# Two modulation slabs in the arena, and small loads, the attention bias, the first output slab and the first transposes moved, in a two-layer block kernel on one core

## The chip, the cores and the metric

The kernel runs on one core of one Trainium2 chip. The metric is the device time of one execution in microseconds (us); the median of the timed runs counts. The profile is one further execution with the hardware profiler. PE is TensorE, DVE is VectorE, ACT is ScalarE, POOL is GpSimd; SyncE (SP) computes nothing and only issues transfers.

## The reference, cut to what matters

The input is a sequence of 256 tokens of 1024 features, float32. Two blocks follow each other.

```
mod = silu(c) @ ada_w + ada_b                     # six rows: shift1, scale1, gate1, shift2, scale2, gate2
h = rms_norm(x, norm_mix_w) * (1 + scale1) + shift1
proj = h @ w_in                                   # attention q, k, v; gated scan q, forget, value, gate; branch gates
x = x + gate1 * ((g0 * (att @ w_branch_att) + g1 * (scan @ w_branch_hg)) @ w_out)
h = rms_norm(x, norm_ffn_w) * (1 + scale2) + shift2
x = x + gate2 * expert_choice_ffn(h)              # 16 experts, 32 tokens each, 1024 x 2048 gate, up and down
# second block: gMLP with spatial gating, squared-ReLU MLP, banded attention with a
# relative bias per head, squared-ReLU MLP
```

## The kernel before, in words

The work is one long hand-written program for each engine, and the engines meet only through semaphores. Weights come in slabs of 2 MB. `FIRST_SLABS` lists the 27 slabs of the stage before the experts in the order in which SyncE issues them: `ada0` to `ada11` are column blocks of the modulation weight, `W0` to `W10` of `w_in`, `att`, `hg`, `out0` and `out1` the branch and output weights. They go round a ring of three slots (`slot_of`, `BEFORE`, line 484 issues them), and a slot is loaded again when the slab three places earlier has been used: for an `ada` slab when TensorE has finished its job, for the others when VectorE has written the low part of its last chunk (`chunk_low`). The 192 expert slabs, 16 KB to each partition, go round six slots; the second three lie where `parts` lay, so they wait for the last product before the experts.

Most products are made in three passes over a high and a low part of both operands. ACT copies a chunk (half a slab) to its rounded high part (line 701), DVE subtracts to get the low part (line 1117, both called by `split_to`), and three chunk buffers are used in turn. `ada` slabs are multiplied as they are: `ada_part` (line 1848) makes four partial rows, DVE copies them out (line 1168), and `ada_col` (line 1858) or `ada_row` (line 1869) sums and turns them. DVE makes `modc` and `aff1` from them (line 1220).

`JOBS` is the order in which TensorE fills PSUM: job i uses bank pair i modulo 4 and waits until job i - 4 has been drained. `norm(0)` transposes the normalised input (line 1760, jobs `nT0a`, `nT0b`). Then `turn_out` scales and shifts it: ACT writes the high part in four quarters (line 743), DVE recomputes each quarter into `tmp`, of which there are two halves (line 1161), and POOL subtracts to get the low part (line 592, `low_parts`). TensorE waits for all four low parts and for the first chunk of `W1`, and starts the projections (lines 1777 to 1779).

At the end of the mixer stage TensorE computes `ya`, `yh` (the branches), `ada10`, the transposes `mT` of the merged rows, `mo0` with `out0`, the row of `ada10`, `ada11`, and `mo1` with `out1`. `mo0` and `mo1` have 48 matrix products each, in two halves of 24. POOL loads the attention bias of the second block (2 MB, line 650) once `yh1` is done. The arena is 64 KB of each partition (`at(kb, columns)`); its first 32 KB are unused until `W1` has been computed.

Before the first slab, SyncE, ACT and POOL issue thirteen small loads for the vectors (lines 490, 491, 492, 688, 574), ACT then `x` and before all of them the constants, and POOL the router weight and three weight rows (lines 578 to 583). SyncE waits for all small vectors before the second slab:

```python
if n == 1:
    sp.wait_ge(vrow_in, 16 * 10)
    sp.wait_ge(vrow_in2, 16 * 3)
```

## Time and profile before

| | us |
|---|---|
| median of 3 timed runs | 1966.03 (1964.84 to 1968.62) |
| the profiled execution, its own time | 1967.66 |
| its span in the trace | 1965.8 |
| chain that ended last: DMA, PE, DVE, ACT | 44%, 43%, 7%, 3% |
| PE busy, DVE busy, ACT busy, POOL busy | 1441.2, 594.1, 487.7, 107.4 |
| transfers, mean | 287 GB/s, 565.12 MB |

An engine's busy time says how much it worked, not what it was worth. The chain that ended last is followed back from the last instruction, at each step to what released it; only what lies on it moves the end. A granted clock of 1.00 is 2.4 GHz and of 0.50 is 1.2 GHz.

### The profile page before, as it was taken

Reading aid. Unit: us, or ns where it says so; the run is one execution under the profiler, and the core shown is the slowest. Engines: PE = TensorE matmul, PEld = TensorE weight load, DVE = VectorE, ACT = ScalarE, POOL = GpSimd, SP = SyncE. Lnnn points to the kernel's source line nnn. Section 1 sums busy time; section 2 is a strip of 40 time slices with the busy share of each in tenths; the row PEclk is TensorE's granted clock in tenths of the full one; section 3 lists DMA queues with packets and bytes.
Section 4 is the critical chain, followed back from the end, with each engine's and each line's share of the span. In section 5 each row is a group of like instructions: output and inputs, shape, how many; then the busy total and the mean of one; then the engine's idle time right before and its main releaser. Section 6 shows DMA issues by size and latency. Waiting matters only on the chain.

```text
span 1965.8 us, 19906 instructions
## 1 busy us (share of the span) xinstructions
PE 1441.2 (73%) x8303; PEld 871.5 (44%) x8303; DVE 594.1 (30%) x677; ACT 487.7 (25%) x636; POOL 107.4 (5%) x93
## 2 busy tenths in 40 slices
PE   4868798666566566566566556559799989879998
PEld 2865576311111111111111111118598879668987
DVE  2475655300000000000000000026545545655554
ACT  3443452200000000000000000034434444544343
POOL 2453200200000000000000000000000000000000
PEclk8978899688877888878878888869799999989999
DMA  9422577499999999999999999985245434314450
GB/s 334 152 86 86 199 252 262 177 428 430 428 428 430 427 428 429 428 428 429 428 428 429 428 428 429 428 341 189 79 180 201 176 129 172 136 57 172 173 198 36
DMA packets 97432, 565.12 MB, mean 287 GB/s; under 512 B 4732, under 2 KB 5896, under 8 KB 72808
## 3 DMA queue, kind: packets, MB, share of 16 engines
q1 hardware_dynamic: 94792, 555.81, 70.0%
q0 software_dynamic: 2112, 7.06, 1.2%
q10 hardware_dynamic: 480, 1.57, 0.2%
q8 instruction: 35, 0.57, 0.1%
q14 instruction: 13, 0.11, 0.0%
HBM read 563.37 MB, written 1.05 MB: 287 GB/s over the span
## 4 chain that ended last, share of the span: by engine, by line
DMA 44%; PE 43%; DVE 7%; ACT 3%; issue 2%; POOL 1%; SPq 0%; DVEq 0%; ACTq 0%; POOLq 0%
DMA ring_b<-in_w_exp_down_dram 22%; DMA ring_b<-in_w_exp_up_dram 20%; PE PS L1777 11%; PE PS L1778 11%; PE PS L1779 11%; PE PS L2080 3%; PE PS L2094 2%; PE PS L1760 1%; DMA ring_a<-in_ada_w_dram 1%; PE PS L1910 1%; DMA ring_a<-in_w_out_dram 1%; DVE parts L1117 1%; DMA ring_a<-in_w_in_dram 1%; DVE arena L1234 1%; POOL hT L592 1%
## 5 line engine op out<-in xcount | busy, mean ns | idle before, releaser
L2080 PE MATMUL PS<-ring_a,arena 128*32 128x512 f32 x1280 | 188.6, 719 | 120.0 <-DMA ring_a<-in_w_exp_up_dram 69.7
L2080 PE MATMUL PS<-ring_b,arena 128*32 128x512 f32 x768 | 128.2, 802 | 98.9 <-DMA ring_b<-in_w_exp_up_dram 63.3
L1777 PE MATMUL PS<-hT,parts 128*128 128x256 f32 x672 | 193.1, 287 | 10.2 <-POOL hT L592 8.0
L2094 PE MATMUL PS<-ring_b,arena 128*32 128x512 f32 x768 | 124.0, 777 | 98.1 <-DMA ring_b<-in_w_exp_down_dram 98.0
L1778 PE MATMUL PS<-hT,parts 128*128 128x256 f32 x672 | 192.4, 286 | 0.0
L1779 PE MATMUL PS<-hT,parts 128*128 128x256 f32 x672 | 192.2, 286 | 0.0
L1506 DVE TENSOR_TENSOR arena<-PS,arena 128x512 f32<-128x512 f32 x16 | 11.1, 692 | 597.5 <-PE PS L2080 597.5
L1117 DVE TENSOR_TENSOR parts<-ring_a,parts 128x2048 fp32r<-128x2048 f32 (+1 forms) x62 | 141.6, 2292 | 110.0 <-ACT parts L701 109.8
L1626 DVE TENSOR_TENSOR parts<-ring_a,parts 128x2048 fp32r<-128x2048 f32 x60 | 137.4, 2292 | 107.4 <-ACT parts L1009 106.8
L2080 PEld LDWEIGHTS PS<-ring_a,arena 128*32 128x32 f32 x1280 | 37.6, 120 | 261.2 <-DMA ring_a<-in_w_exp_up_dram 110.8
L701 ACT ACTIVATE parts<-ring_a 128x2048 fp32r<-128x2048 f32 (+1 forms) x62 | 116.6, 1890 | 142.2 <-PE PS L1779 107.9
L1009 ACT ACTIVATE parts<-ring_a 128x2048 fp32r<-128x2048 f32 x60 | 114.7, 1912 | 114.6 <-PE PS L1779 114.6
L1777 PEld LDWEIGHTS PS<-hT,parts 128*128 128x128 f32 x672 | 131.3, 195 | 13.2 <-POOL hT L592 8.4
L1778 PEld LDWEIGHTS PS<-hT,parts 128*128 128x128 f32 x672 | 131.3, 195 | 0.5
L1779 PEld LDWEIGHTS PS<-hT,parts 128*128 128x128 f32 x672 | 131.3, 195 | 0.0
L1779 PE MATMUL PS<-parts,rounded 128*128 128x512 f32 x320 | 126.8, 396 | 0.0
L1778 PE MATMUL PS<-parts,rounded 128*128 128x512 f32 x320 | 126.8, 396 | 0.0
L1777 PE MATMUL PS<-parts,rounded 128*128 128x512 f32 x320 | 126.8, 396 | 0.0
L1777 PE MATMUL PS<-parts,hT 128*128 128x512 f32 (+1 forms) x288 | 116.2, 403 | 10.9 <-issue 7.1
L1778 PE MATMUL PS<-parts,hT 128*128 128x512 f32 (+1 forms) x288 | 114.3, 397 | 0.0
L2080 PEld LDWEIGHTS PS<-ring_b,arena 128*32 128x32 f32 x768 | 24.2, 128 | 202.5 <-DMA ring_b<-in_w_exp_up_dram 104.0
L1779 PE MATMUL PS<-parts,hT 128*128 128x512 f32 (+1 forms) x288 | 113.8, 395 | 0.0
(284 smaller groups left out, 1651.1 us busy)
## 6 DMA issues: line engine op xcount, KB each, us to landing
ring_a<-in_w_exp_gate_dram SPq DMA_DIRECT2D x48, 2048.0 KB, 25.8
ring_b<-in_w_exp_down_dram SPq DMA_DIRECT2D x48, 2048.0 KB, 26.2
ring_b<-in_w_exp_up_dram SPq DMA_DIRECT2D x32, 2048.0 KB, 26.2
ring_a<-in_w_exp_up_dram SPq DMA_DIRECT2D x32, 2048.0 KB, 25.6
ring_b<-in_w_exp_gate_dram SPq DMA_DIRECT2D x16, 2048.0 KB, 27.1
ring_a<-in_w_exp_down_dram SPq DMA_DIRECT2D x16, 2048.0 KB, 26.6
ring_a<-in_w_up_dram SPq DMA_DIRECT2D x16, 2048.0 KB, 8.6
ring_a<-in_w_down_dram SPq DMA_DIRECT2D x16, 2048.0 KB, 7.6
```

The source lines that it names most:

```text
L592: pool.tensor_tensor(low, tmp[:, b * NB:(b + 1) * NB], high.bitcast(F32), ALU.subtract)\
L701: act.activation(part_of(c, 0), raw(c), ACT.Copy).then_inc(chunk_high, 1)
L1009: act.activation(part_of(c, 0), raw(c), ACT.Copy).then_inc(chunk_high, 1)
L1117: dve.tensor_tensor(part_of(c, 1), raw(c), part_of(c, 0).bitcast(F32), ALU.subtract)\
L1234: dve.tensor_tensor(split(dst, s)[side], split(dst, s)[side], split(src, s)[side], ALU.mult)
L1626: dve.tensor_tensor(part_of(c, 1), raw(c), part_of(c, 0).bitcast(F32), ALU.subtract)\
L1760: ins = nc.tensor.transpose(bank(job, i // 4)[:, (i % 4) * P:(i % 4 + 1) * P], src, ident)
L1777: mm(out, left[0], right[0], start=start, stop=False)
L1778: mm(out, left[0], right[1], start=False, stop=False)
L1779: return mm(out, left[1], right[0], start=False, stop=stop)
L2080: ins = mm(PS[32 * j:32 * j + 32, side, :], xe[:, 2 * q + kk, :], w[:, kk, j * NB:(j + 1) * NB], start=q == 0 and kk == 0, stop=q == 3 and ...
L2094: ins = mm(PS[32 * q:32 * q + 32, 2 + n, :], hidT[:, q, 32 * i:32 * i + 32], w[:, q, n * NB:(n + 1) * NB], start=i == 0, stop=i == 3)
```

## The change

`ada0` and `ada1` get two slots of their own in the arena, and the ring of three starts with `ada2`; so the first five slabs are issued one behind the other, and SyncE no longer waits for the small vectors. ACT loads the identity first (64 KB) and the rest of the constants (425 KB) after `x`, with two semaphores in place of one. POOL issues the router weight and the three weight rows after the low parts of `nT0`. TensorE makes `adc1` and `adc2` earlier and the transposes `norm(0)` before `ada3`. ACT and DVE split the first chunk of `W1` after the turn-out of `nT0` and not before it, and the forget-gate bounds are computed after the first norm. `out0` is loaded before `ada10`; `ada11` is computed right behind `ada10`, before the transposes `mT`. The attention bias is loaded after the experts, behind the first of four norm rows.

```diff
--- before.py
+++ after.py
@@ -46,15 +46,15 @@
...
     [("vecT", 1)]
-    + [(j, 1) for j in ("ada0", "ada1", "adc0", "ada2", "adc1", "ada3", "adc2", "adc3")]
-    + [("nT0a", 2), ("nT0b", 2)]
+    + [(j, 1) for j in ("ada0", "ada1", "adc0", "adc1", "ada2", "adc2")]
+    + [("nT0a", 2), ("nT0b", 2), ("ada3", 1), ("adc3", 1)]
     + [("W1", 2), ("W2", 2), ("W0", 2), ("lv0", 2), ("W4", 2), ("lv1", 2), ("W5", 2), ("lv2", 2), ("W3", 2)]
...
     + [("adr4", 1), ("adr5", 1), ("ohgT", 2), ("W9", 2), ("W10", 2), ("ya0", 2), ("ya1", 2), ("yh0", 2), ("yh1", 2)]
-    + [("ada10", 1), ("mTa", 2), ("mTb", 2), ("mo0", 2), ("adr10", 1), ("ada11", 1), ("mo1", 2), ("adr11", 1)]
+    + [("ada10", 1), ("ada11", 1), ("mTa", 2), ("mTb", 2), ("mo0", 2), ("adr10", 1), ("mo1", 2), ("adr11", 1)]
     + [("nT1a", 2), ("nT1b", 2), ("rt", 1), ("rl", 1), ("aT", 1), ("ic", 1), ("ib", 1)]
@@ -75,7 +75,7 @@
...
     + [("ada4", "ada4"), ("ada5", "ada5"), ("W9", "W9"), ("W10", "W10"), ("att", "ya1"), ("hg", "yh1")]
-    + [("ada10", "ada10"), ("out0", "mo0"), ("ada11", "ada11"), ("out1", "mo1")]
+    + [("out0", "mo0"), ("ada10", "ada10"), ("ada11", "ada11"), ("out1", "mo1")]
 )
@@ -134,13 +134,15 @@
...
+    if n < 2:
+        return R + n
     if n < AT_EXPERT:
-        return n % RS
+        return (n - 2) % RS
     return (n - AT_EXPERT) % R if n < AT_A else (n - AT_A) % RS
-ARRIVED, BEFORE, _count, _last = [], [], [0] * R, [None] * R
+ARRIVED, BEFORE, _count, _last = [], [], [0] * (R + 2), [None] * (R + 2)
 for _n in range(AT_FFN[1] + 2 * FJ):
@@ -290,13 +292,14 @@
...
         psum_drained = [sem(f"psum_drained{i}") for i in range(4)]
-        slab_in = [sem(f"slab_in{i}") for i in range(R)]
+        slab_in = [sem(f"slab_in{i}") for i in range(R + 2)]
         chunk_high, chunk_low = sem("chunk_high"), sem("chunk_low")
...
         slab_done = sem("slab_done")
-        consts_in, x_in, rows_in, wr_in = (sem(n) for n in ("consts_in", "x_in", "rows_in", "wr_in"))
+        ident_in, tables_in, x_in, rows_in, wr_in = (
+            sem(n) for n in ("ident_in", "tables_in", "x_in", "rows_in", "wr_in"))
@@ -359,6 +362,8 @@
...
             i = slot_of(n)
+            if i >= R:
+                return at(16 * (i - R), SLOT)
             return ring_a[:, i, :] if i < RS else ring_b[:, i - RS, :]
@@ -493,10 +498,6 @@
...
                 n = SLAB_AT[name]
-                if n == 1:
-
-                    sp.wait_ge(vrow_in, 16 * 10)
-                    sp.wait_ge(vrow_in2, 16 * 3)
                 if name.startswith("ada"):
@@ -574,14 +575,6 @@
...
             link(pool.memset(wr[:, :, :], 0.0))
-            for a in range(2):
-                pool.dma_start(wr.rearrange("p (q a) e -> p q a e", a=2)[:, :, a, 0:NE],
-                               A["w_router"][0].rearrange("(q p a) e -> p q a e", p=P, a=2)[:, :, a]).then_inc(wr_in, 16)
-
-            pool.dma_start(wqk[:, 0:64], A["q_norm_w"][0].partition_broadcast(P)).then_inc(rows_in, 16)
-            pool.dma_start(wqk[:, 64:128], A["k_norm_w"][0].partition_broadcast(P)).then_inc(rows_in, 16)
-            pool.dma_start(hgw[:, :], A["hg_norm_w"][0].partition_broadcast(P)).then_inc(rows_in, 16)
-
             def low_parts(jobs):
@@ -593,6 +586,14 @@
...
             low_parts(("nT0a", "nT0b"))
+
+            for a in range(2):
+                pool.dma_start(wr.rearrange("p (q a) e -> p q a e", a=2)[:, :, a, 0:NE],
+                               A["w_router"][0].rearrange("(q p a) e -> p q a e", p=P, a=2)[:, :, a]).then_inc(wr_in, 16)
+
+            pool.dma_start(wqk[:, 0:64], A["q_norm_w"][0].partition_broadcast(P)).then_inc(rows_in, 16)
+            pool.dma_start(wqk[:, 64:128], A["k_norm_w"][0].partition_broadcast(P)).then_inc(rows_in, 16)
+            pool.dma_start(hgw[:, :], A["hg_norm_w"][0].partition_broadcast(P)).then_inc(rows_in, 16)
@@ -627,6 +628,7 @@
             pool.wait_ge(rows_in, 48)
+            pool.wait_ge(tables_in, 16)
             pool.wait_ge(qk_rstd, 1)
@@ -645,12 +647,6 @@
...
-
-            wait_full(pool, "yh1")
-            pool.dma_start(bias[:, :, :], hankel(A["b_rel_bias_2"])).then_inc(bias_in, 16)
-            pool.wait_ge(bias_in, 16)
-
-            pool.memset(bias[0:64, :, 0:64], NEG).then_inc(bias_masked, 1)
@@ -679,14 +675,19 @@
...
                 pool.dma_start(grows[n], row.partition_broadcast(P)).then_inc(grow_in[n % 2], 16)
+                if n == 0:
+                    pool.dma_start(bias[:, :, :], hankel(A["b_rel_bias_2"])).then_inc(bias_in, 16)
+                    pool.wait_ge(bias_in, 16)
+                    pool.memset(bias[0:64, :, 0:64], NEG).then_inc(bias_masked, 1)
...
         def _(act):
-            act.dma_start(consts[:, :], A["consts"]).then_inc(consts_in, 16)
+            act.dma_start(ident, A["consts"][:, C_ID:C_ID + P]).then_inc(ident_in, 16)
             for v, src in VECTORS[4:8]:
...
             act.dma_start(x[:, :, :], A["x"][0].rearrange("(t p) d -> p t d", p=P)).then_inc(x_in, 16)
+            act.dma_start(consts[:, P:C_END], A["consts"][:, P:C_END]).then_inc(tables_in, 16)
@@ -751,14 +752,13 @@
...
             act.wait_ge(lb_in, 1)
-            act.activation(small[:, 24:32], small[:, 16:24], ACT.Exp).then_inc(lb_exp, 1)
             act.activation(csil[:, :], vcol[:, V_C:V_C + 8], ACT.Silu).then_inc(c_silu, 1)
...
                 root(0, t)
-            split_to(0)
+            act.activation(small[:, 24:32], small[:, 16:24], ACT.Exp).then_inc(lb_exp, 1)
             act.wait_ge(aff_ready, 1)
@@ -1197,30 +1197,29 @@
...
             ins.then_inc(crep_ready, 1)
+            for t in range(T):
+                mean_square(0, t)
+            for t in range(T):
+                rescale(0, t)
             dve.wait_ge(lb_exp, 1)
...
             dve.tensor_scalar(small[:, 8:16], small[:, 0:8], -1.0, 1.0, ALU.mult, ALU.add).then_inc(lb_ready, 1)
-            for t in range(T):
-                mean_square(0, t)
-            for t in range(T):
-                rescale(0, t)
             ada_part(0)
...
             ada_col(0)
+            ada_col(1)
             ada_part(2)
-            ada_col(1)
+            ada_col(2)
             ada_part(3)
-            ada_col(2)
             ada_col(3)
...
             dve.wait_ge(aff_ready, 1)
-            split_to(0)
             turn_out(("nT0a", "nT0b"), aff1, modc)
@@ -1256,6 +1255,7 @@
...
             dve.tensor_tensor(EK, gkf, gkb, ALU.add).then_inc(factors_ready, 1)
+            dve.wait_ge(tables_in, 16)
             scores(0)
@@ -1413,6 +1413,7 @@
...
             ada_part(10)
+            ada_part(11)
             wait_drained(dve, "adc9")
@@ -1431,7 +1432,6 @@
...
             ada_row(10, gate2[:, 0:NB])
-            ada_part(11)
@@ -1868,7 +1868,7 @@
...
-            pe.wait_ge(consts_in, 16)
+            pe.wait_ge(ident_in, 16)
             pe.wait_ge(vrow_in, 16 * 10)
@@ -1881,12 +1881,12 @@
...
             ada_col(0)
+            ada_col(1)
             ada_part(2)
-            ada_col(1)
+            ada_col(2)
+            norm(0)
             ada_part(3)
-            ada_col(2)
             ada_col(3)
-            norm(0)
             pe.wait_ge(low_out, 4)
@@ -1998,13 +1998,13 @@
...
             ada_part(10)
+            ada_part(11)
             pe.wait_ge(merged_ready, 4)
...
             ada_row(10)
-            ada_part(11)
             natural_by_tile("mo1", hT)
@@ -2021,6 +2021,7 @@
...
             wait_drained(pe, "rt")
+            pe.wait_ge(tables_in, 16)
             for t in range(T):
```

## Rows read from the trace of the kernel before

**Rows 1.** Chain in order of time, expert stage: start, length (us), what, count.

```profile
385.43 10.48 PE PS L2080 x96
...
1274.47 27.41 DMA ring_b<-in_w_exp_down_dram
```

**Rows 2.** Timeline, 0 to 60 us, all engines.

```profile
11.44 0.61 ACT L713 ACTIVATE junk<-x 128x512 bf16<-128x512 f32 x1
...
17.20 0.72 ACT L722 ACTIVATE xn<-x,rstd 128x512 f32<-128x512 f32 x1 [0.23 <-DVE rstd L1130]
...
25.33 1.05 PE L1858 MATMUL PS<-mean,arena 128*128 128x1 f32 x8
...
28.99 3.41 PE L1848 MATMUL PS<-ring_a,crep 128*32 128x512 f32 x16 [2.60 <-DMA ring_a<-in_ada_w_dram]
...
34.41 2.67 PE L1848 MATMUL PS<-ring_a,crep 128*32 128x512 f32 x16 [1.03 <-DMA ring_a<-in_ada_w_dram]
...
37.01 3.58 PE L1858 MATMUL PS<-mean,arena 128*128 128x1 f32 x16
37.13 0.69 DVE L1168 COPY arena<-PS 128x512 f32<-128x512 f32 x1 [3.54 <-PE PS L1848]
...
40.45 3.65 PE L1760 MATMUL PS<-consts,xn 128*128 128x128 f32 x16
...
40.82 0.17 DVE L1220 SCALAR_TENSOR_TENSOR aff<-modc,vcol 128x8 f32<-128x8 f32 x1
...
42.49 3.75 ACT L743 ACTIVATE hT<-PS,modc,aff 128x256 fp32r<-128x256 f32 x8 [0.86 <-PE PS L1760]
43.95 1.90 DVE L1161 TENSOR_SCALAR tmp<-PS,aff,modc 128x256 f32<-128x256 f32 x4
```

**Rows 3.** Chain in order of time, around 52 us.

```profile
52.08 0.58 PE PS L1777
```

**Rows 4.** Busy time by stretch; last columns granted clock, DMA share, GB/s.

```profile
9.00:15.00 6.00, 0.00 (x0) 0.00 (x0) 1.92 (x16) 5.85 (x13) 0.00 (x0) 1.00 1.00 186
20.00:25.00 5.00, 3.31 (x28) 0.47 (x20) 0.69 (x1) 0.00 (x0) 0.00 (x0) 1.00 1.05 387
330.00:332.00 2.00, 2.00 (x6) 1.58 (x5) 1.97 (x5) 0.72 (x2) 0.00 (x0) 0.50 1.01 434
...
1325.00:1330.00 5.00, 2.98 (x7) 2.46 (x8) 4.95 (x7) 2.75 (x4) 0.00 (x0) 0.50 0.00 0
```

**Rows 5.** DMA queues, 10 to 15 us: packets, MB, share of 16 engines.

```profile
q0 software_dynamic: 84, 0.11, 55.3%
```

**Rows 6.** GpSimd's subtractions of line 592: duration ns min/median/max, first and last start.

```profile
L592 POOL TENSOR_TENSOR hT<-tmp,hT x4: 1261/1262/3303, 45.0 to 48.7; 128x512 fp32r<-128x512 f32 x4
```

**Rows 7.** VectorE's low parts, line 1117, 48 to 54 us, same columns.

```profile
L1117 DVE TENSOR_TENSOR parts<-ring_a,parts x2: 2361/2852/3344, 48.5 to 50.8; 128x2048 fp32r<-128x2048 f32 x2
```

**Rows 8.** GpSimd's timeline.

```profile
67.84 2.16 POOL L603 TENSOR_SCALAR arena<-arena,small 128x256 f32<-128x256 f32 x4 [15.82 <-ACT arena L772]
```

**Rows 9.** Timeline of PE, 304 to 343 us.

```profile
305.54 1.92 PE L1848 MATMUL PS<-ring_a,crep 128*32 128x512 f32 x16
308.32 1.97 PE L1760 MATMUL PS<-consts,xn 128*128 128x128 f32 x16 [0.86 <-DVE xn L1412]
312.67 0.47 PE L1777 MATMUL PS<-parts,hT 128*128 128x512 f32 x1 [2.38 <-issue]
...
323.67 1.03 PE L1869 MATMUL PS<-arena,mean 128*128 128x512 f32 x2
...
328.96 0.73 PE L1777 MATMUL PS<-parts,hT 128*128 128x512 f32 x1 [2.41 <-DVE parts L1117]
...
341.54 1.02 PE L1869 MATMUL PS<-arena,mean 128*128 128x512 f32 x2
```

**Rows 10.** Chain in order of time, 305 to 330 us.

```profile
307.52 14.83 DMA ring_a<-in_w_out_dram
```

**Rows 11.** DMA issues, 305 to 340 us: count, KB each, us to landing.

```profile
arena<-in_b_rel_bias_dram POOLq DMA_DIRECT2D x1, 2048.0 KB, 12.6
```

## The prediction

> **What bounds the kernel now.** I read the page first: its chain is 44% transfers and 43% TensorE, so there are stages with different limits. The chain in order of time separates them. From 385.43 us, when TensorE opens the first expert, to 1301.88 us (1274.47 + 27.41) each step is the arrival of an expert slab [rows 1]: a stream of fixed length, 916.4 us, that starts when TensorE frees the first slot. Behind it lie 663.9 us to the end of the span, which the change touches at one place only. So a microsecond won before 385.43 is one won at the end, and what counts is the chain before it. There it is led by TensorE and its partners, with two stretches in which a transfer sets the pace: the start, up to `W1`'s first product at 52.08 [rows 3], where the timeline of all engines shows TensorE taking each modulation slab as it lands [rows 2]; and `out1`, for which the chain waits 14.83 us from 307.52 [rows 10]. The change works on these two.
>
> **The start, part one: when the slabs land.** From 20 to 25 us the transfers run at 387 GB/s, from 9 to 15 us at 186 [rows 4]. That is 6.0 x (387 - 186) = 1206 KB less, or 3.1 us at 387. In 10 to 15 us POOL's queue has 84 packets of 0.11 MB but 55.3% of the engines' time [rows 5]; these are the router weight and the three rows, which now leave this window. Their 0.2 MB gives another 0.5 us. Sum 3.6 us: `ada2`, taken at 28.99 [rows 2], then lands at 25.4. The bounds are 0 (the hole has another cause) and 3.6. The missing wait of SyncE before `ada1`, the two arena slots and the earlier issues are costed at nothing: the transfer engines are full from 20 us on, so a deeper queue moves no byte sooner. The constants bring the same bytes in another order.
>
> **Part two: TensorE from `ada2` to `aff1`.** Before, `aff1` is written at 40.82 + 0.17 = 40.99 [rows 2], after `ada3` (34.41), its copy, and `adc2` with `adc3` (3.58 for both). Now TensorE does, from 25.4: `ada2`, copy, `adc2`, 16 transposes, `ada3`, copy, `adc3`, and DVE's sum and `aff1`. An `ada` part took 3.41 and 2.67 here [rows 2] and 1.92 later [rows 9]; one column job 1.05 or 3.58 / 2 = 1.79; the transposes 3.65 here and 1.97 later; a copy 0.69, 0.75 with its hand-overs [rows 2]; the last two 0.35. These pairs are the two levels of TensorE's clock, and it was changing between them here, so I take the middle: 2.67 + 0.75 + 1.4 + 2.8 + 2.67 + 0.75 + 1.4 + 0.35 = 12.8, hence 38.2. All fast gives 9.8 (35.2), all slow 3.41 + 0.75 + 1.79 + 3.65 + 3.41 + 0.75 + 1.79 + 0.35 = 15.9 (41.3). The transposes stand in front of `ada3` and delay it beyond its landing at 30.8; that price is in the sum. The normalised input was complete at 17.92 [rows 2], so they don't wait for it.
>
> **Part three: from `aff1` to `W1`.** Before this takes 52.08 - 40.99 = 11.1. ACT started its turn-out at 42.49, released by the transposes; these are now done, so it starts 0.07 behind `aff1` and saves 1.4. Its first quarter was done at 42.49 + 3.75 / 4 = 43.43, and DVE began only at 43.95 [rows 2], behind the low part of `W1`'s first chunk; that split is moved, so 0.5 more goes. What remains is 11.1 - 1.9 = 9.2. But the moved split meets POOL's last quarter: three of POOL's subtractions took 1.26 us and the one beside DVE's split 3.30 [rows 6], while of DVE's two splits the first took 2.36 and the second 3.34 [rows 7]: each waited for the other's whole instruction. Before, a split lay there too, so the 9.2 holds it: DVE finishes the turn-out 5.7 behind ACT's start, and then 2.36 of split and 1.26 of POOL stand in a row in either order, ending at 9.2 to 9.4. The Trainium skill has this as a rule that speaks against moving the split (SBUF — State Buffer, on the shared port pair): the pair is an exclusive lock, and the second of the two engines fully blocks. By that rule the trace agrees; without a lock the stage would take 8.1, 1.1 less. `W1` then starts at 38.2 + 9.2 = 47.4, a gain of 4.7 (7.7 all fast, 1.6 all slow; with no earlier landings 1.1 in the middle and -2.0 all slow).
>
> Other edits at the start cost nothing: the exponential for the forget bounds and DVE's four steps of it are due at POOL's work at 67.84, before which POOL idled 15.82 [rows 8]; the same gap covers the five issues on POOL, and SyncE's queue isn't behind them. The waits for the rest of the constants come long after these land. If the gap were gone, POOL's issues would cost 3 us. From 52 to 305 us the order is unchanged and the chain passes through no transfer, so the gain is carried whole; a microsecond may be lost where POOL and DVE meet otherwise.
>
> **The end of the mixer stage** (times as before, unshifted). TensorE makes `ada10` from 305.54 and the transposes `mT` from 308.32. With `ada11` (1.92) behind `ada10` they start at 305.54 + 2 x 1.9 = 309.35, 1.03 later. `mo0` moves from 312.67 to 313.70 and its row job from 323.67 to 324.70; then comes `mo1`, 1.0 later, at 325.7, where before it started at 328.96 [rows 9]. It took 12.58 (to 341.54), `mo0` 11.00 for the same 48 products; the granted clock was 0.50 in 330 to 332 [rows 4], after TensorE had waited 2.41. Without that wait I take 11.00, so `mo1` ends at 336.7, 4.8 us earlier.
>
> Is `out1` there in time? It now waits for the low part of `out0`'s last chunk (written at 304.9, as before) and not for `ada10`, which gives 2.6. It was in flight for 14.83 [rows 10], beside the bias, 2 MB in 12.6 [rows 11]. Even at 14.83 it lands at 319.7. Both halves, high and low, took from 322.35 to 328.96, 6.6: ready at 326.3, and `mo1` would start 0.6 later. I take no delay, since the bias is gone. The second half of `out1` waits for a chunk buffer that `mo0`'s first half frees at 313.70 + 5.5 = 319.2; one half of the 6.6 less DVE's other split is 4.2, ready at 323.4, under 325.7. Gain 4.8; bounds 3.3 (clock low as before) and 4.8. The expert slabs behind `out1` have some 50 us to land.
>
> **The bias, now behind the experts.** POOL issues it near 1318 us; at 12.6 it lands by 1331, and the transfer engines moved nothing from 1325 to 1330 [rows 4]. The slab after that is used tens of us later and the bias at 1696. POOL's mask is one memset of 1 us; it could block one split on DVE, at most 1 us, with no one waiting. Cost 0, upper bound 1.
>
> **Sum.** 4.7 + 4.8 = 9.5 us. The profiled execution had 1965.8 of span and 1967.66 in all; it becomes 1956.3 of span and 1958.2. It lay 1.6 above the median of 1966.03, so the median becomes 1956.5.
>
> **Rivals.**
> 1. *The start gives little.* The hole at 9 to 15 us isn't POOL's traffic, or the clock stays low through the transposes. The start gives 1.1 to 1.6, the sum is 6.1, the time 1959.9. For it: the granted clock fell in this stretch before, and half of the hole has few POOL packets. Against: the queue's 55.3%.
> 2. *The start at full clock.* TensorE has less idle between its jobs; 7.7 + 4.8 = 12.5, the time 1953.5.
> 3. *`mo1` gains little:* `out1` is late for another reason, 4.8 becomes 1, the time 1960.3. Against it stand the 2.3 us of slack.
> 4. *Slower: `x` arrives behind the five slabs.* The old order kept `ada1` back until the small vectors were in. If the transfer engines now serve five queued slabs before ACT's queue, `x` lands with `W1`, near 36; its norm took 6.5 (11.44 to 17.92 [rows 2]), and then 16 transposes at 2.8, `ada3` 2.67, copy, `adc3` and 0.35 put `aff1` at 50.5 and `W1` at 59.7: 7.6 later, less 4.8, so 2.8 slower net, 1968.8; with the clock low as well, up to 1972. The transposes wait from the point at which `x` lands after 24; the start's gain is gone at 28, and the kernel is slower from 33. Against: `x` was here by 11.44 beside a queued slab.
>
> The Trainium skill has a rule on this (DMA: Bandwidth & Descriptors, on queues, rings and completion order): each transfer engine goes round-robin over the queues it has work for. By that rule this rival does not happen; no run here has shown five slabs queued.
>
> **How the numbers follow.** Forecast (start 3 to 6.5, end 3.3 to 4.8) 0.57; rival 1 0.20; rival 2 0.10; rival 3 0.07; rival 4 and unforeseen waits 0.06. The range reaches to rival 2 and past rival 1: 1952.8 to 1961.5. A change within 0.2% (3.9 us) is what a measurement can't tell from none. Faster by more: all of the forecast and rival 2, most of 1 and 3, 0.89; the same 0.07; slower 0.04.
>
> **What would show it.** The new profile should have the modulation slabs taken near 14.5, 20 and 25.4; no 186 GB/s in 9 to 15; transposes ahead of the last `ada` part; one long POOL subtraction still; `W1` from 45 to 50; no wait for `out1` ahead of `mo1`, about 11 us for `mo1`; the first expert near 375.9; the slab stream still 916 us; nothing waiting on POOL near 1320. The prediction is wrong if the stream's length changes, if the gain of the start is eaten between 52 and 305, or if the hole stays.

## The result and the profile after

The changed kernel takes 1953.07 us in the median of 9 runs, against 1966.03 in 9 runs of the kernel before: ratio 0.9933, 95% interval 0.9915 to 0.995. Timed again later it gave 1958.36 (6 runs) against 1967.76, ratio 0.9948, interval 0.9935 to 0.996. By the ratios the change is worth 10.2 and 13.2 us, by the medians 9.4 and 13.0, where 9.5 (a time of 1956.5) was forecast; the median of all 15 runs of the changed kernel is 1955.49. The profiled execution took 1949.28 with a span of 1947.5. It is 3.8 us under the median, and the one of before was 1.6 over; the difference of 18.3 us between the two traces is therefore more than the change gives, and part of this study is to say which of it is the change.

The timeline of the changed kernel's first 50 us (start, length, engine, line, output and input) answers to [rows 2 and 3]. The slabs `ada0` to `ada3` are multiplied at 14.57, 19.89, 25.54 and 31.13:

```profile
8.97 0.63 ACT L714 ACTIVATE junk<-x 128x512 bf16<-128x512 f32 x1 [0.78 <-DMA x<-in_x_dram]
...
14.57 3.64 PE L1848 MATMUL PS<-arena,crep 128*32 128x512 f32 x16 [8.78 <-DMA arena<-in_ada_w_dram]
...
19.89 3.64 PE L1848 MATMUL PS<-arena,crep 128*32 128x512 f32 x16 [1.67 <-DMA arena<-in_ada_w_dram]
...
25.54 1.92 PE L1848 MATMUL PS<-ring_a,crep 128*32 128x512 f32 x16
...
29.25 1.95 PE L1760 MATMUL PS<-consts,xn 128*128 128x128 f32 x16
...
31.13 1.92 PE L1848 MATMUL PS<-ring_a,crep 128*32 128x512 f32 x16
...
35.21 0.17 DVE L1220 SCALAR_TENSOR_TENSOR aff<-modc,vcol 128x8 f32<-128x8 f32 x1
35.41 3.76 ACT L744 ACTIVATE hT<-PS,modc,aff 128x256 fp32r<-128x256 f32 x8 [18.43 <-DVE aff L1220]
...
44.75 0.58 PE L1777 MATMUL PS<-hT,parts 128*128 128x256 f32 x1 [9.78 <-POOL hT L585]
```

Four things are to be seen here: `ada2` is multiplied 3.5 us earlier than in [rows 2]; the transposes (line 1760) stand ahead of the last `ada` part and take the short duration; the turn-out is released by `aff1` itself, 0.03 behind it; and `x` is in time, at 8.97. The busy time in 9 to 15 us (granted clock, DMA share and GB/s last) shows the hole filled, against [rows 4]:

```profile
9.00:15.00 6.00, 0.43 (x4) 0.23 (x8) 1.70 (x8) 5.42 (x13) 0.00 (x0) 1.00 1.04 390
```

One caution for reading the granted clock: that column says 1.00 from the start of the span, also while TensorE is idle, and it still says 1.00 while `ada0` and `ada1` take 3.64, the duration that goes with 0.50 elsewhere (u2's `ada2`: 3.64 at 0.50). Ahead of the first fall in a profile, the durations tell the level and the column does not.

The instructions of GpSimd's and VectorE's lines in the same stretch (minimum, median, maximum in ns), as in [rows 6 and 7]:

```profile
L585 POOL TENSOR_TENSOR hT<-tmp,hT x4: 1260/1264/3316, 37.7 to 41.4; 128x512 fp32r<-128x512 f32 x4
```

```profile
L1117 DVE TENSOR_TENSOR parts<-ring_a,parts x3: 2278/2369/3357, 41.2 to 46.8; 128x2048 fp32r<-128x2048 f32 x3
```

One of four subtractions is long and so is one of three splits, as before. At the end of the mixer stage TensorE's timeline answers to [rows 9]: both `ada` parts together (x32), and `mo1` right behind the row job of `ada10`.

```profile
297.56 3.64 PE L1848 MATMUL PS<-ring_a,crep 128*32 128x512 f32 x32
...
316.48 1.02 PE L1869 MATMUL PS<-arena,mean 128*128 128x512 f32 x2
316.94 0.79 PE L1777 MATMUL PS<-parts,hT 128*128 128x512 f32 x1
...
328.27 1.02 PE L1869 MATMUL PS<-arena,mean 128*128 128x512 f32 x2
```

And the chain in order of time, for the expert stage [rows 1]:

```profile
370.88 12.18 PE PS L2081 x96
...
1262.15 25.63 DMA ring_b<-in_w_exp_down_dram
```

The stream of slabs takes 916.9 us (to 1287.78), against 916.4. Set beside each other, in us:

| stretch | before | after | difference |
|---|---|---|---|
| start to `W1` | 52.08 | 44.75 | -7.3 |
| `W1` to `ada10` | 253.5 | 252.8 | -0.7 |
| `ada10` to the end of `mo1` | 36.0 | 30.7 | -5.3 |
| end of `mo1` to the first expert | 43.9 | 42.6 | -1.3 |
| slab stream | 916.4 | 916.9 | +0.5 |
| last expert slab to the end | 663.9 | 659.7 | -4.2 |

The two stretches on which the change works give 12.6. The other rows differ as much between executions of kernels that are alike there, as the experiments show. In the row from `mo1` to the first expert this is again TensorE's clock: it is 42.6 to 42.7 in the six profiles with the new end in which the 16 transposes of the second norm take 2.2, and 44.7 in the three (e3, u3, c1) in which they take 3.69.

### The profile page after: what moved, and what is told of

It reads as the page before. It is cut to its first block, busy times and chain, and to the rows that moved or that the text cites. A ratio compares the mean times of both kernels' runs of the same rounds, so it can differ in the third digit from the quotient of the medians.

```text
span 1947.5 us, 19908 instructions
## 1 busy us (share of the span) xinstructions
PE 1440.6 (74%) x8303; PEld 865.2 (44%) x8303; DVE 594.5 (31%) x677; ACT 488.2 (25%) x636; POOL 107.3 (6%) x93
## 4 chain that ended last, share of the span: by engine, by line
PE 45%; DMA 43%; DVE 7%; ACT 3%; issue 2%; POOL 1%; SPq 0%; DVEq 0%; ACTq 0%; POOLq 0%
DMA ring_b<-in_w_exp_down_dram 21%; DMA ring_b<-in_w_exp_up_dram 20%; PE PS L1777 11%; PE PS L1778 11%; PE PS L1779 11%; PE PS L2081 3%; PE PS L2095 2%; PE PS L1760 1%; DMA arena<-in_ada_w_dram 1%; PE PS L1910 1%; PE PS L1848 1%; DVE arena L1233 1%; POOL hT L585 1%; DVE arena L1234 1%; ACT junk L714 0%
## 5 line engine op out<-in xcount | busy, mean ns | idle before, releaser
L2081 PE MATMUL PS<-ring_b,arena 128*32 128x512 f32 x768 | 130.6, 816 | 101.2 <-DMA ring_b<-in_w_exp_up_dram 64.8
L2095 PE MATMUL PS<-ring_b,arena 128*32 128x512 f32 x768 | 129.6, 809 | 92.0 <-DMA ring_b<-in_w_exp_down_dram 91.9
L1506 DVE TENSOR_TENSOR arena<-PS,arena 128x512 f32<-128x512 f32 x16 | 11.1, 691 | 596.4 <-PE PS L2081 596.4
L2081 PEld LDWEIGHTS PS<-ring_a,arena 128*32 128x32 f32 x1280 | 38.2, 122 | 256.6 <-DMA ring_a<-in_w_exp_up_dram 105.4
L1777 PEld LDWEIGHTS PS<-hT,parts 128*128 128x128 f32 x672 | 131.0, 195 | 14.7 <-POOL hT L585 9.9
L1777 PE MATMUL PS<-parts,hT 128*128 128x512 f32 (+1 forms) x288 | 114.4, 397 | 8.4 <-issue 7.1
L2081 PEld LDWEIGHTS PS<-ring_b,arena 128*32 128x32 f32 x768 | 24.4, 130 | 205.1 <-DMA ring_b<-in_w_exp_up_dram 105.2
L2095 PEld LDWEIGHTS PS<-ring_b,arena 128*32 128x32 f32 x768 | 24.2, 130 | 199.1 <-DMA ring_b<-in_w_exp_down_dram 155.8
L1778 PE MATMUL PS<-parts,hT 128*128 128x512 f32 (+1 forms) x288 | 112.6, 391 | 0.0
```

What stands on the lines that cost most here:

```text
L1777: mm(out, left[0], right[0], start=start, stop=False)
L1778: mm(out, left[0], right[1], start=False, stop=False)
L2081: ins = mm(PS[32 * j:32 * j + 32, side, :], xe[:, 2 * q + kk, :], w[:, kk, j * NB:(j + 1) * NB], start=q == 0 and kk == 0, stop=q == 3 and ...
L2095: ins = mm(PS[32 * q:32 * q + 32, 2 + n, :], hidT[:, q, 32 * i:32 * i + 32], w[:, q, n * NB:(n + 1) * NB], start=i == 0, stop=i == 3)
```

## The experiments

Four kernels carry one part of the change each on the kernel before (e1 to e4), five undo one part of it or its order in the changed kernel (u1 to u5), one is the changed kernel again (c1), and two try something further (k1, k2). Each was timed in several rounds beside the kernel before and profiled once. The table has the milestones of the profiles (us) and the ratio of the times to the kernel before, with its interval. The `ada2` column is the start of its products, `aff1` the end of its write, and `W1` the first product.

| kernel | `ada2` | `aff1` | `W1` | `W1` to `ada10` | `ada10` to end of `mo1` | last slab to end | ratio |
|---|---|---|---|---|---|---|---|
| before | 28.99 | 40.99 | 52.08 | 253.5 | 36.0 | 663.9 | 1 |
| e1, GpSimd's loads late | 24.98 | 37.96 | 48.71 | 256.1 | 34.3 | 659.8 | 0.9986 (0.9977 to 0.9994) |
| e2, order of the start and split | 29.80 | 44.10 | 53.39 | 256.3 | 34.2 | 659.9 | 0.9989 (0.9978 to 1.0) |
| e3, order of the end | 29.71 | 39.39 | 52.81 | 253.6 | 30.7 | 661.5 | 0.9964 (0.995 to 0.9978) |
| e4, bias late | 29.78 | 41.86 | 52.9 | 253.4 | 32.0 | 657.7 | 0.9978 (0.9967 to 0.999) |
| after | 25.54 | 35.38 | 44.75 | 252.8 | 30.7 | 659.7 | 0.9933 (0.9915 to 0.995) |
| u1, GpSimd's loads early | 30.53 | 41.66 | 50.96 | 255.9 | 30.7 | 662.6 | 0.996 (0.9943 to 0.9977) |
| u2, bias early | 25.33 | 39.18 | 48.55 | 252.9 | 30.7 | 659.1 | 0.9939 (0.9921 to 0.9956) |
| u3, split first | 25.36 | 35.19 | 49.87 | 253.8 | 30.7 | 658.5 | 0.996 (0.9941 to 0.9978) |
| u4, no arena slots | 25.33 | 36.46 | 45.82 | 255.8 | 30.7 | 662.7 | 0.9938 (0.9918 to 0.9958) |
| u5, old order of the start | 25.43 | 37.56 | 48.39 | 253.5 | 30.7 | 656.3 | 0.9937 (0.9924 to 0.995) |
| c1, the changed kernel again | 25.40 | 39.69 | 49.05 | 253.9 | 30.7 | 661.5 | 0.9948 (0.9935 to 0.996) |
| k1, TensorE kept busy, start | 26.48 | 40.22 | 55.75 | 253.4 | 30.7 | 659.5 | 0.997 (0.9957 to 0.9983) |
| k2, the same at six places | 26.70 | 38.21 | 53.75 | 253.4 | 30.7 | 664.5 | 0.9991 (0.9983 to 1.0) |

**e1: GpSimd's four loads behind the low parts, in the kernel before.**

```diff
             link(pool.memset(wr[:, :, :], 0.0))
-            for a in range(2):
-                pool.dma_start(wr..., A["w_router"]...).then_inc(wr_in, 16)
-            pool.dma_start(wqk[:, 0:64], ...); pool.dma_start(wqk[:, 64:128], ...); pool.dma_start(hgw[:, :], ...)
...
             low_parts(("nT0a", "nT0b"))
+            (the same loads)
```

> The kernel before with one part of the change: GpSimd issues the router weight and the three weight rows behind the low parts of nT0. Theory (the traffic of these four loads makes the hole of 186 GB/s in 9 to 15 us): the hole is filled, ada2 is taken near 25.5 instead of 28.99, W1's first product comes 3 to 4 us earlier, near 48.5, and the time falls by 3 to 4 us. Rival (the hole comes from SyncE's wait for the small vectors before ada1, which is kept here): the hole stays, ada2 is taken at 29, the time is unchanged.

The hole is gone while SyncE's wait before `ada1` is still there; busy time by stretch in e1:

```profile
9.00:15.00 6.00, 0.85 (x5) 0.26 (x9) 1.92 (x16) 5.85 (x13) 0.00 (x0) 1.00 1.05 392
```

`ada2` is taken at 24.98, 4.0 us before [rows 2], and `W1` starts 3.4 earlier, at 48.71. The median falls by 4.0 us (1964.37 against 1968.38), by the ratio of the runs 2.8 (1.2 to 4.5). The rival, that the wait makes the hole, is out.

**u1: the same loads early, in the changed kernel.** 

```diff
             link(pool.memset(wr[:, :, :], 0.0))
+            (the loads of wr, wqk and hgw, as in the kernel before)
...
             low_parts(("nT0a", "nT0b"))
-            (the same loads)
```

> The changed kernel with the router weight and the three weight rows issued at the start again, as in the kernel before. Theory: the hole is back although SyncE doesn't wait for the vectors, ada2 lands 3 to 3.6 us later than in the changed kernel, W1 starts near 48.5 instead of 44.75. Rival (the hole was SyncE's wait or the order of the constants): the slabs land as in the changed kernel, W1 at 45.

The hole is back without SyncE's wait, and with it GpSimd's queue; the stretches and the queues from 10 to 15 us in u1:

```profile
9.00:15.00 6.00, 0.00 (x0) 0.00 (x0) 1.35 (x7) 5.20 (x12) 0.00 (x0) 1.00 0.97 159
```

```profile
q0 software_dynamic: 94, 0.13, 61.4%
q1 hardware_dynamic: 193, 0.40, 26.6%
```

`ada2` is at 30.53 and `W1` at 50.96. The median is 1960.15, beside 1953.09 and 1953.64 for u2 and u4 in the same rounds. The first slab is multiplied at 19.69, 1.5 us later than in the kernel before too, so the loss is 5 us of landing, not 3.6. Both directions agree: these 0.2 MB of loads put the slabs off by 4 to 5 us. In this stretch a packet of GpSimd's queue held a transfer engine for 0.52 us (an estimate: 61.4% of 16 engines in 5 us, over 94 packets) and one of SyncE's queue for 0.11. Whether that comes from the small pieces of the router weight, from the broadcast of the three rows or from GpSimd's queue as such was not tried. The Trainium skill (DMA: Bandwidth & Descriptors, Queues, rings and completion order) has each transfer engine go round the queues that have work, a whole packet at a time; by that rule the small loads get turns although slabs are queued ahead of them, and the trace agrees: GpSimd's queue moved 94 packets beside 193 of SyncE's. Why a turn with so few bytes is so long, the rule doesn't say and no run here shows.

**e2: the new order of the start and the late split, in the kernel before.**

```diff
-    + [(j, 1) for j in ("ada0", "ada1", "adc0", "ada2", "adc1", "ada3", "adc2", "adc3")]
-    + [("nT0a", 2), ("nT0b", 2)]
+    + [(j, 1) for j in ("ada0", "ada1", "adc0", "adc1", "ada2", "adc2")]
+    + [("nT0a", 2), ("nT0b", 2), ("ada3", 1), ("adc3", 1)]
...
-            split_to(0)
             act.wait_ge(aff_ready, 1)
...
-            split_to(0)
             turn_out(("nT0a", "nT0b"), aff1, modc)
```

> The kernel before with the new order of TensorE and VectorE at the start (adc1, adc2 and the transposes ahead of ada3) and the first split behind the turn-out; loads as before. Theory: slabs are taken at the same times as before, aff1 stands near 38 to 40.5 by the clock, the turn-out starts at once behind it, from aff1 to W1 takes 9.2 to 9.4 instead of 11.1, W1 starts at 47.5 to 50, and the time falls by 2 to 4.5 us. Rival (the transposes ahead of ada3 cost what they save): aff1 is at or beyond 41, W1 at 50.3 or later, the time falls by less than 2.

In the profile this is a miss: `aff1` at 44.10 and `W1` at 53.39, later than before. TensorE's timeline in e2 shows why:

```profile
29.80 2.77 PE L1846 MATMUL PS<-ring_a,crep 128*32 128x512 f32 x16 [0.17 <-DMA ring_a<-in_ada_w_dram]
33.45 1.84 PE L1856 MATMUL PS<-mean,arena 128*128 128x1 f32 x8 [0.88 <-DVE arena L1167]
35.15 3.65 PE L1758 MATMUL PS<-consts,xn 128*128 128x128 f32 x16
38.74 3.02 PE L1846 MATMUL PS<-ring_a,crep 128*32 128x512 f32 x16
```

The column job took 1.84 and the transposes 3.65, so `ada3`, landed near 35, began at 38.74. The granted clock was 0.62 in 30 to 33 and 0.50 in 33 to 39. From `aff1` to `W1` it took 9.3, as forecast. So this profile shows what the rival said. Over the timed executions the part is worth 2.2 us by the ratio, and the interval (0 to 4.3) holds both the expectation and the rival: the times don't decide between them.

**u5: TensorE's and VectorE's old order, in the changed kernel** (the split stays late).

```diff
+            ada_part(2)
             ada_col(1)
-            ada_part(2)
+            ada_part(3)
             ada_col(2)
-            norm(0)
-            ada_part(3)
             ada_col(3)
+            norm(0)
```

> The changed kernel with TensorE's and VectorE's old order at the start (transposes behind ada3 and its columns, adc1 and adc2 late), the loads and the late split as in the changed kernel. Theory: ada3 is taken when it lands, 30.8; aff1 is at 34.5 to 36, not later than in the changed kernel, but the turn-out waits for the transposes and starts 1.0 to 2.5 us behind aff1; W1 at 45.5 to 47.5, the time 0.5 to 2 us above the changed kernel. Rival (the early transposes are worth what they were costed at, 1.4 us and more): W1 at 47.5 or later.

`aff1` at 37.56, the turn-out 1.50 behind it, `W1` at 48.39, beyond the 47.5 of the rival; but `ada2`, `ada3` and the transposes ran at 3.34, 2.80 and 3.65 here. The turn-out in u5, released by PE:

```profile
37.39 0.17 DVE L1220 SCALAR_TENSOR_TENSOR aff<-modc,vcol 128x8 f32<-128x8 f32 x1
39.06 3.76 ACT L744 ACTIVATE hT<-PS,modc,aff 128x256 fp32r<-128x256 f32 x8 [22.12 <-PE PS L1760]
```

The ratio is 0.9937, that of the changed kernel. The early transposes take 1.5 us off the way from `aff1` to `W1`, and they put `ada3` back: TensorE began it at 30.85 in u5, and in the kernels with the new order and the same slabs at 30.93 and 31.13 (u3 and the changed kernel, clock at 1.00 throughout) to 34.60 and 34.92 (c1 and u2, where the clock was at 0.50 ahead of it). What they save is thus lost again where the clock is low. Timed, they are worth nothing that shows.

**u3: the first split ahead of the turn-out again, in the changed kernel.**

```diff
+            split_to(0)
             act.wait_ge(aff_ready, 1)
...
+            split_to(0)
             turn_out(("nT0a", "nT0b"), aff1, modc)
```

> The changed kernel with the first split of W1 ahead of the turn-out again on ScalarE and VectorE. W1's slab landed near 43 minus the split in the changed kernel, at about 36. Theory: ScalarE waits for W1 (about 36.3), splits 1.9, and the turn-out starts at 38.2 instead of 35.4, VectorE's share of the split 2.3 ends at 40.5, so W1's first product is 3 to 3.5 us later, 48. Rival (VectorE's split in GpSimd's way costs as much as it saves): W1 within 1 us of 44.75.

The timeline of u3 from `aff1` on:

```profile
35.02 0.17 DVE L1221 SCALAR_TENSOR_TENSOR aff<-modc,vcol 128x8 f32<-128x8 f32 x1
37.45 1.91 ACT L702 ACTIVATE parts<-ring_a 128x2048 fp32r<-128x2048 f32 x1 [20.38 <-DMA ring_a<-in_w_in_dram]
39.26 3.75 ACT L744 ACTIVATE hT<-PS,modc,aff 128x256 fp32r<-128x256 f32 x8
39.46 2.29 DVE L1118 TENSOR_TENSOR parts<-ring_a,parts 128x2048 fp32r<-128x2048 f32 x1 [4.27 <-ACT parts L702]
```

ACT waits for `W1` to land, 37.4, then splits, and the turn-out starts 4.1 behind `aff1`. `W1`'s first product is at 49.87, 14.7 behind `aff1`, against 9.4 in the changed kernel: 5.3 us, more than the 3.5 expected, because DVE's half of the split comes on top (1.2). The median is 1957.38, 4 us above u2 and u4 in the same rounds, and the ratio, 0.996 against 0.9933 and 0.9948, points to 2.4 to 5.3 us; but the intervals of these kernels touch, so it is the trace that shows this part and not the time alone.

The same wait was there in the kernel before. Its chain in order of time, from `ada1` on, passes not through TensorE and `aff1` but through the landing of `W1` and its split:

```profile
25.46 14.23 DMA ring_a<-in_w_in_dram
...
39.72 1.92 ACT parts L701
...
41.74 2.29 DVE parts L1117
44.03 0.92 DVE tmp L1161 x2
```

From the start of ACT's split to `W1`'s first product it took 12.36 us here (39.72 to 52.08), 12.36 in e3 (from 40.45), 12.35 in e4 (from 40.51) and 12.42 in u3 (from 37.45), although `aff1` was anywhere from 2.3 us ahead of the split's start (u3) to 1.4 behind it (e4). Only in e1, where the transposes ran at the low clock and held the turn-out to 39.47, it took 13.0. With the split in front, the landing of `W1` thus sets the start, or the transposes come within 0.6 us of doing so; with the split behind, `aff1` does.

**u4: no arena slots, and SyncE's wait back, in the changed kernel.**

```diff
-    if n < 2:
-        return R + n
     if n < AT_EXPERT:
-        return (n - 2) % RS
+        return n % RS
...
+                if n == 1:
+                    sp.wait_ge(vrow_in, 16 * 10)
+                    sp.wait_ge(vrow_in2, 16 * 3)
```

> The changed kernel with the ring of three for all slabs and SyncE's wait for the vectors, so without the arena slots. Theory (the transfer engines are the limit, a deeper queue moves no byte sooner): the slabs are taken at the same times within 0.5 us, W1 starts at 44.8 to 45.5, the time is that of the changed kernel. Rival (the two more slots let ada3 and W1 be issued in time): ada3 or W1 lands 1 us or more later and the start loses it.

The slabs are taken at 14.49, 19.82 and 25.33, as with the slots, `W1` at 45.82, and the median is 1953.64 (ratio 0.9938). The slots are worth nothing. They do let SyncE issue sooner: `ada3` at 10.69 in the changed kernel and at 18.05 in u4, `W1` at 16.26 and at 21.81. But the slabs land at the same times. These are the transfers of `W1` in the changed kernel and in u4, from issue to landing:

```profile
ring_a<-in_w_in_dram SPq DMA_DIRECT2D x1, 2048.0 KB, 21.3
```

```profile
ring_a<-in_w_in_dram SPq DMA_DIRECT2D x1, 2048.0 KB, 15.6
```

`W1` lands at 37.6 and 37.4, and `ada3` at 30.7 in both (10.69 + 20.0 and 18.05 + 12.6). The transfer engines are busy throughout (390 and 393 GB/s in 9 to 15 us, 387 in 20 to 25), so an earlier issue only waits longer, as the prediction had it. Part of that wait is on SyncE itself. In the changed kernel the third slab's issue took 6.62 us and the fourth's 5.53; `ada3`'s took 0.37 in u4.

```profile
4.03 6.62 SPq L489 DMA_DIRECT2D ring_a<-in_ada_w_dram  x1
```

**e3: the order of the end, in the kernel before.**

```diff
-    + [("ada10", "ada10"), ("out0", "mo0"), ("ada11", "ada11"), ("out1", "mo1")]
+    + [("out0", "mo0"), ("ada10", "ada10"), ("ada11", "ada11"), ("out1", "mo1")]
...
             ada_part(10)
+            ada_part(11)
             pe.wait_ge(merged_ready, 4)
...
             ada_row(10)
-            ada_part(11)
```

> The kernel before with out0 loaded before ada10 and ada11 computed behind ada10; the bias stays where it was. Theory (the order is what frees mo1, the bias alone makes out1 slow): out1 is issued near 305 and lands 13 to 15 us later, mo1 starts at 325.7 to 327 instead of 328.96 and runs in 11.0 to 11.3, so it ends near 337.2 and the time falls by 4 to 4.8. Rival (the bias is what holds mo1, whatever the order): mo1 starts at 328 or later, the time falls by less than 1.5.

With the bias where it was, `ada10` to the end of `mo1` takes 30.7 instead of 36.0; the two row jobs on TensorE in e3 lie 11.79 apart:

```profile
325.35 1.02 PE L1869 MATMUL PS<-arena,mean 128*128 128x512 f32 x2
...
337.14 1.02 PE L1869 MATMUL PS<-arena,mean 128*128 128x512 f32 x2
```

`out1` took 10.7 beside the bias, which itself took 24.9. The time falls by 7.1 by the ratio; the interval, 4.3 to 9.8, holds the 5.3 of the stretch.

**e4: the bias behind the experts, in the kernel before.**

```diff
-            wait_full(pool, "yh1")
-            pool.dma_start(bias[:, :, :], hankel(A["b_rel_bias_2"])).then_inc(bias_in, 16)
-            pool.wait_ge(bias_in, 16)
-            pool.memset(bias[0:64, :, 0:64], NEG).then_inc(bias_masked, 1)
...
+                if n == 0:
+                    (the same, behind the first norm row)
```

> The kernel before with the attention bias loaded behind the experts and nothing else changed. Theory (the bias stretches out1's transfer, and ada11 stands between mo0 and mo1): out1, issued at 307.5, lands in 8 to 11 instead of 14.83, mo1 starts right behind ada11 near 326.6 and ends near 337.7, the time falls by about 4. Rival (out1's lateness comes from its issue time, not from the bias): out1 still takes 13 or more, mo1 starts at 328.5 or later, the time is unchanged. Behind the experts neither expects a wait for the bias: from the last expert slab's landing to the end within 2 us of 663.9.

`out1` lands in 7.6 in place of 14.83 and `ada10` to the end of `mo1` takes 32.0: 4.0 less, as expected.

```profile
ring_a<-in_w_out_dram SPq DMA_DIRECT2D x1, 2048.0 KB, 7.6
```

The time falls by 4.3 by the ratio (2.0 to 6.5). So the rival, that only the issue time makes `out1` late, is out: with the bias gone, `out1` lands in half the time. From the last expert slab to the end it takes 657.7, so behind the experts the bias costs nothing that shows.

**u2: the bias early again, in the changed kernel.**

```diff
+            wait_full(pool, "yh1")
+            (the load of the bias, its wait and its mask)
...
                 if n == 0:
-                    (the same)
```

> The changed kernel with the bias loaded at yh1 again. Theory (order and bias each give most of the end's gain, so undoing one loses little): out1 is issued 0.3 us behind the end of the yh products, takes 13 to 15, and mo1 starts 0 to 1.5 us later relative to ada10 than in the changed kernel. Rival (the gain of the end is the bias's): mo1 starts 3 us or more later and the time is 4 us above the changed kernel.

`ada10` to the end of `mo1` takes 30.7 as in the changed kernel, although `out1` needs 10.9 in place of 7.7; the ratio is 0.9939. With the new order there is slack for the bias, and moving it as well adds nothing that shows.

**c1: the changed kernel again.**

> The changed kernel once more, to see how one execution's stretches differ from another's. Theory (the slabs' arrivals are fixed, what varies is the level of TensorE's clock): ada2 taken at 25.3 to 25.6 as before; aff1 anywhere from 35.2 to 39.3, the later the more of ada2, adc2, the transposes and ada3 run at the double duration; from ada10's start to the end of mo1's products 30.7 again; slab stream 916 to 917.5. Rival (the arrivals vary): aff1 late together with late slabs.

The slabs are taken at the same times, within 0.15 us, up to `ada2`, and `aff1` is at 39.69, 4.3 later than in the first profile. TensorE's timeline in c1, and its stretches (PE busy first, granted clock third from the end):

```profile
19.90 3.27 PE L1848 MATMUL PS<-arena,crep 128*32 128x512 f32 x16 [1.69 <-DMA arena<-in_ada_w_dram]
...
25.40 3.04 PE L1848 MATMUL PS<-ring_a,crep 128*32 128x512 f32 x16 [0.30 <-DMA ring_a<-in_ada_w_dram]
29.32 1.84 PE L1858 MATMUL PS<-mean,arena 128*128 128x1 f32 x8 [0.88 <-DVE arena L1168]
31.02 3.65 PE L1760 MATMUL PS<-consts,xn 128*128 128x128 f32 x16
34.60 2.75 PE L1848 MATMUL PS<-ring_a,crep 128*32 128x512 f32 x16
```

```profile
26.00:27.00 1.00, 1.00 (x11) 0.27 (x4) 0.00 (x0) 0.00 (x0) 0.00 (x0) 0.54 1.06 389
...
27.00:30.00 3.00, 2.12 (x12) 0.71 (x4) 0.69 (x1) 0.00 (x0) 0.00 (x0) 0.50 1.05 384
```

27 to 30 us in the first profile of the same kernel:

```profile
27.00:30.00 3.00, 2.10 (x23) 1.67 (x16) 0.85 (x2) 0.00 (x0) 0.00 (x0) 1.00 1.05 385
```

The clock was 0.50 in one execution and 1.00 in the other, with the same slabs at the same times. `ada2`, the transposes and `ada3` took 3.04, 3.65 and 2.75 instead of 1.92, 1.95 and 1.92, and `W1` came at 49.05 instead of 44.75: 4.3 us, all of it of this kind. Ahead of the fall the two executions differ in little: in c1 `ada1` took 3.27 where the first profile has 3.64, TensorE then waited 0.30 for `ada2`, where it had no gap in the first profile, and the clock fell just after 26 us. No run shows whether these small differences decide it. The first trace was in any case a favourable one.

**k1: TensorE kept busy at the start.** If the clock falls while TensorE waits for slabs, products that nobody reads might hold it up. 50 float32 products of the identity (128 x 128) stand ahead of `ada0`, 72 behind `adc3`.

```diff
+            def warm(job, n, dst=None):
+                if job:
+                    begin(job)
+                    dst = bank(job, 0)[:, 0:P]
+                for _ in range(n):
+                    mm(dst, ident, ident, start=True, stop=True)
...
+            warm("ada0", 50)
             pe.wait_ge(crep_ready, 1)
...
             ada_col(3)
+            warm(None, 72, bank("ada3", 1)[:, 0:P])
             pe.wait_ge(low_out, 4)
```

> The changed kernel with products that nobody reads in two idle stretches of TensorE: 50 of 128 columns ahead of ada0 and 72 behind adc3, before W1. Theory (TensorE's clock level, and not the slabs, is what is left of the start's scatter): granted clock 1.00 from ada0 to the end of W1; all ada parts at 1.92, aff1 at 35.2 to 35.6; W1's first 18 products at 0.12 us and not 0.21; 1.7 us against the best execution and 2 to 4 in the median against the changed kernel. Rival (the extra products hold TensorE up or the clock falls all the same): W1 starts later than 45.5 or its first products take 0.21; the time is unchanged or higher.

A miss, first by its size. TensorE's timeline in k1:

```profile
5.55 12.61 PE L1877 MATMUL PS<-consts 128*128 128x128 f32 x100
...
18.09 1.92 PE L1848 MATMUL PS<-arena,crep 128*32 128x512 f32 x16
...
20.97 1.92 PE L1848 MATMUL PS<-arena,crep 128*32 128x512 f32 x16 [0.95 <-DMA arena<-in_ada_w_dram]
...
26.48 3.64 PE L1848 MATMUL PS<-ring_a,crep 128*32 128x512 f32 x16 [1.66 <-DMA ring_a<-in_ada_w_dram]
...
39.67 16.32 PE L1877 MATMUL PS<-consts 128*128 128x128 f32 x144
```

Each product is two records (x100 for 50) and takes 0.23 to 0.25 us. The second block therefore ran to 55.75, where `W1`, by the usual 9.3 behind `aff1` (40.22), was due at 49.5: some 6 us were lost to the block itself. The first block also held `ada0` back, from 14.57 to 18.09. It did raise the level at first: `ada0` and `ada1` took 1.92 each, where the changed kernel has 3.64. But then the clock fell all the same. After `ada0` and `ada1`, with a wait of 0.95 between them, and a wait of 1.66 behind the column jobs, it was 0.53 in 25 to 30 us:

```profile
25.00:30.00 5.00, 3.52 (x16) 0.69 (x16) 0.02 (x1) 0.00 (x0) 0.00 (x0) 0.53 1.05 386
```

Being busy without a gap from 5 to 18 us did not keep the clock at 26. `W1`'s products lay 0.12 apart from 55.95 on, but from `W1` to `ada10` it took 253.4, no less than in the changed kernel. The median is 1961.79, 3.4 above c1 in the same rounds. Whether smaller blocks closer to the work would gain was not tried.

**k2: the same, and such blocks around the norms later in the kernel.** The edit is that of k1 with `warm(...)` of 16 to 72 products ahead of and behind `norm(1)` to `norm(5)`.

> As the run before, with such products also in the idle stretches around the transposes of the five later norms (16 or 44 around norm(1), 72 and 16 around norm(2), 44 and 16 around norm(3) and norm(5), 60 and 16 around norm(4)). Theory: the 16 transposes of each norm take 1.9 us and not 3.7, and the first products behind them run at full clock; 3 to 4 us at each of norm(2) to norm(5) and 1 at norm(1), so the part behind the slab stream falls from 658 to 664 us to 645 to 650, and the time by 10 to 14 us against the changed kernel. Rival (the products delay the norm's own work, or the chip throttles): the part behind the stream stays above 655.

A miss too. The block ahead of `norm(2)` ran 16.34 us, and the transposes behind it were fast, at 1.91 where the changed kernel has 3.65:

```profile
1308.40 16.34 PE L1877 MATMUL PS<-consts 128*128 128x128 f32 x144
1324.58 1.91 PE L1760 MATMUL PS<-consts,xn 128*128 128x128 f32 x16
1326.33 3.74 PE L1877 MATMUL PS<-consts 128*128 128x128 f32 x32
```

But from the last expert slab to the next product of real work it took 30.3 us (1299.54 to 1329.86), against 23.5 in the changed kernel (1287.78 to 1311.30). The stretch grew by 6.8 us for the 1.7 us that the transposes saved; the median, 1966.11, is near that of before. None of these kernels beats the changed one; u2, u4 and u5 equal it.

## Why the prediction was right, point by point

**Where the slabs land.** 3.6 us were forecast, and both directions confirm place and cause: 25.54 instead of 28.99 in the profile, 4.0 in e1, 5.0 in u1. The removed wait and the arena slots were costed at nothing, for the reason that the transfer engines are full, and u4 shows both.

**TensorE from `ada2` to `aff1`.** 12.8 us with bounds of 9.8 and 15.9 put `aff1` at 38.2. The first profile showed the lower bound (35.38), c1 came out at 39.69. Over the profiles that leave the start's order and loads whole (after, u2, u4, c1) `aff1` is at 35.38, 39.18, 36.46 and 39.69, mean 37.7; in those with the old start (before, e3, e4) at 40.99, 39.39 and 41.86, mean 40.7. That is 3.0 of gain, where 2.8 was forecast, out of a scatter of 4 us that the bounds had right. It is the landing that gives it: `ada2` comes 4 us earlier, and the early transposes don't show in the time (u5).

**From `aff1` to `W1`.** 9.2 was forecast; it took 9.37 in the changed kernel, 9.3 in e2. One long subtraction on GpSimd (3316 ns beside 1260) and one long split on VectorE (3357 beside 2278) are there as before. The Trainium skill (SBUF — State Buffer, on the shared port pair) calls the pair an exclusive lock that is held for a whole instruction; the trace agrees with these four numbers. The term that the runs give another size is the moved split, booked at 0.5. That is what it cost in the kernel before behind the late transposes: ACT's turn-out began at 42.49, and DVE was free only at 44.03. But `W1` had landed only at 39.7 there, 1.3 ahead of `aff1`, and the chain of that trace passes through this landing and the split. The prediction took the path over TensorE and `aff1` for the one that sets the start; the two were within 0.6 us of each other. Had the split stayed in front, `aff1`'s earlier place would have gained nothing beyond the landing of `W1`, and u3 puts the moved split at 5.3 us. The new stretch of 9.2 holds no split in front of the turn-out, so its length was right; the share that each edit has in it was not. This also shows in the old stretch, which is 11.1, 13.4 and 11.0 (before, e3, e4): where `aff1` was early, it only waited longer.

**The end of the mixer stage.** 4.8 was forecast and 5.3 is in the profiles, 36.0 to 30.7. `mo1` takes 11.3 (316.94 to its row job at 328.27), where 11.0 was reckoned, and starts without a wait, 0.46 behind the row job of `ada10`, where 1.0 was reckoned. The new value is the same 30.7 in every kernel with the new order. The old one is 36.0, 34.3 and 34.2 (before, e1, e2). Before, `mo1` waited 2.4 and then ran partly at a granted clock of 0.50, 12.6 in all; in e1 it was `mo0` that ran partly at the low clock (0.59 in 312 to 316), and `mo1` waited 0.7 and took 11.0. So the part is worth 3.5 to 5.3, and 4.1 in the mean: within the bounds (3.3 to 4.8) but for the trace of before. What the forecast did not say is that its two edits cover for each other. The order alone gives all of it (e3), the bias alone 4.0 (e4), and both together no more than the order (u2).

**The bias behind the experts.** Costed at nothing; in the changed kernel it landed in 11.4 us, and the stretch behind the experts did not grow in e4 (657.7).

**The rest.** The stream stayed at its length (916.9 and, over all kernels, 916.2 to 917.4). From `W1` to `ada10` the kernels lie between 252.8 and 256.3, from the last slab to the end between 656.3 and 664.5, with no order in either that follows the edits. The 4.2 us that this last stretch lacks after the change is of that size, and its means are 660.8 with the change (after, u2, u4, c1) and 661.0 without (before, e3, e4), so it isn't credited to the change. By the means, `W1` comes at 47.0 with the change and at 52.6 without, 5.5 us where 4.7 was forecast; the end gives 4.1 where 4.8 was forecast. The sum, 9.7, lies beside the 9.5 partly because these two deviations cancel. The ratios say 10.2 and 13.2. The stretch from `mo1` to the first expert, shorter by 0.9 in the mean, is the only other one that follows; what makes up the rest was not located, and it is no larger than the scatter of these stretches.

**The rivals.** Rival 1 fails with the hole filled (e1), though its slow clock does occur (c1). Rival 2, the start at full clock from `ada2` on, is what the first profile shows, and the first median, 1953.07, is nearer to its 1953.5, given a chance of 0.10, than to the forecast's 1956.5; it lies 0.3 inside the low end of the range, which was luck. The second median, 1958.36, lies on the other side of the forecast. The executions mix the two. Rival 3 fails, `mo1` has no wait. Rival 4 fails: ACT's squares of `x` began at 8.97, while SyncE had issued two slabs and was issuing the third. Of the signs given for the new profile, two were missed in the first trace by going further the same way: `W1` at 44.75 (45 to 50 was given) and the first expert at 370.88 (375.9). The others were there. But c1 shows that `W1`'s place in one trace, 44.75 or 49.05, says less than the landing of the slabs and the distance from `aff1`.

**What stays open** is when the clock falls. c1 and the first profile differ ahead of 26 us in 0.37 us of `ada1` and in a wait of 0.30, and k1 only excludes that a busy stretch 8 us earlier prevents the fall. Open too is which property of GpSimd's loads makes them so dear.
